# Row sums of a softmax: eight probability tiles added on GpSimd, and one group of narrow matmuls fewer

## The reference, cut to what is computed

```python
def one_block(qblk):
    s = jnp.einsum('bqkgd,bskd->bkgqs', qblk, k).astype(jnp.float32) * scale
    p = jax.nn.softmax(s, axis=-1).astype(v.dtype)
    return jnp.einsum('bkgqs,bskd->bqkgd', p, v)
```

## Time and profile before

| what | value |
|---|---|
| median of 3 runs | 3239.37 us (3236.63 to 3240.04) |
| span of the profiled execution | 3236.2 us |
| mean granted TensorE clock | 0.973 |
| TensorE busy | 3079.7 us (95%) |
| VectorE busy | 1814.2 us (56%) |
| ScalarE busy | 992.9 us (31%) |
| GpSimd busy | 414.4 us (13%) |
| additions on GpSimd (L709) | 96 |
| narrow matmuls, records on L2025 | 1048 |

### The profile page before, as it was taken

How to read it: one execution, slowest core, us unless ns; L and a number is a source line. 1 busy time by engine, 2 the same in 40 slices (tenths; PEclk the granted TensorE clock), 3 DMA queues, 4 the chain that set the end, 5 groups by cost and what they waited for, 6 DMA issues and landing times.

```text
span 3236.2 us, 44976 instructions
## 1 busy us (share of the span) xinstructions
PE 3079.7 (95%) x17016; PEld 2535.1 (78%) x17016; DVE 1814.2 (56%) x3358; ACT 992.9 (31%) x1913; POOL 414.4 (13%) x605
## 2 busy tenths in 40 slices
PE   5999979999999999999979999899989999999998
PEld 4788855567888888889968888555679998899987
DVE  4446677755745444544475376777457445544457
ACT  3223235435311121112253223444352212122212
POOL 0012333311000000000020023343110000000002
PEclk7999989999999999999999999899999999999999
DMA  5430220002322222221112102200121101101111
GB/s 219 154 126 29 79 78 0 0 27 77 94 70 87 74 83 73 84 79 66 36 62 77 54 16 77 78 0 0 32 82 60 53 27 53 52 27 53 40 40 72
DMA packets 94507, 201.25 MB, mean 62 GB/s; under 512 B 13041, under 2 KB 13681, under 8 KB 93809
## 3 DMA queue, kind: packets, MB, share of 16 engines
q1 hardware_dynamic: 78240, 151.76, 14.8%
q0 software_dynamic: 16080, 46.96, 4.2%
HBM read 181.59 MB, written 17.08 MB: 61 GB/s over the span
## 4 chain that ended last, share of the span: by engine, by line
PE 62%; issue 24%; DVE 7%; DMA 2%; ACT 2%; DVEq 1%; POOL 1%; ACTq 1%; POOLq 0%; SPq 0%
PE ps L1805 15%; PE ps L1808 14%; PE ps L1809 14%; PE ps L2025 6%; PE ps L1996 3%; PE ps L2015 2%; PE ps L2016 2%; PE ps L1787 1%; DVE nm L1509 1%; DMA w_raw<-in_w_slots 1%; PE ps L1923 1%; DVE w_lo L499 1%; DMA modw<-in_w_mod 1%; PE ps L1918 1%; DMA w_raw<-in_m_slots 1%
## 5 line engine op out<-in xcount | busy, mean ns | idle before, releaser
L1805 PE MATMUL ps<-hi,w_hi 128*128 128x384 f32 x1584 | 540.4, 341 | 21.8 <-DVEq L437 9.9
L1809 PE MATMUL ps<-hi,w_lo 128*128 128x384 f32 x1584 | 534.0, 337 | 0.0
L1808 PE MATMUL ps<-lo,w_hi 128*128 128x384 f32 x1584 | 533.6, 337 | 0.0
L494 ACT CAST w_hi<-w_raw 128x512 fp32r<-128x512 f32 x368 | 213.8, 619 | 767.8 <-PE ps L1805 720.3
L1805 PE MATMUL ps<-w_hi,hi 128*128 128x512 f32 (+1 forms) x1008 | 389.4, 386 | 7.3 <-ACT stg L810 4.1
L1808 PE MATMUL ps<-w_lo,hi 128*128 128x512 f32 (+1 forms) x1008 | 381.3, 378 | 0.0
L1809 PE MATMUL ps<-w_hi,lo 128*128 128x512 f32 (+1 forms) x1008 | 381.3, 378 | 0.0
L1668 DVE TENSOR_TENSOR ps<-ps,gate 128x512 f32<-128x512 f32 x288 | 201.0, 698 | 261.4 <-PE ps L1809 261.0
L1805 PE MATMUL ps<-w_hi,f_hi 128*128 128x512 f32 x864 | 342.6, 397 | 0.0
L1808 PE MATMUL ps<-w_lo,f_hi 128*128 128x512 f32 x864 | 337.0, 390 | 0.0
L1809 PE MATMUL ps<-w_hi,f_lo 128*128 128x512 f32 x864 | 336.6, 390 | 0.0
(11 more groups left out here) (299 smaller groups left out, 4758.5 us busy)
## 6 DMA issues: line engine op xcount, KB each, us to landing
w_raw<-in_w_slots SPq DMA_DIRECT2D x368, 256.0 KB, 3.4
w_raw<-in_m_slots SPq DMA_DIRECT2D x160, 256.0 KB, 2.8
out<-xr POOLq DMA_DIRECT2D x18, 512.0 KB, 3.2
modw<-in_w_mod SPq DMA_DIRECT2D x4, 2048.0 KB, 15.8
acc<-in_x_in SPq DMA_DIRECT2D x3, 1536.0 KB, 22.6
zq_dram<-stg POOLq DMA_DIRECT2D x18, 256.0 KB, 2.4
xr<-in_x_in POOLq DMA_DIRECT2D x2, 2304.0 KB, 9.3
xr<-out POOLq DMA_DIRECT2D x2, 2304.0 KB, 9.8
```

The costliest lines, as they stand in the source:

```text
L494: act.copy(w_hi[:, j, :], w_raw[:, j % RAW, :]).then_inc(S["w_hi_done"], 1)
L1805: mm = pe.matmul(out, a_hi, b_hi, start=first, stop=False)
L1808: pe.matmul(out, a_hi, b_lo, start=False, stop=False)
L1809: return pe.matmul(out, a_lo, b_hi, start=False, stop=last)
```

## The change

- GpSimd adds tiles 0 to 7 into `psm`, seven additions a step in place of three (`SUMS` = 7). Additions 1 to 4 stand ahead of the four diagonals one by one, 5 to 7 behind the last diagonal.
- `row_sums` is gone. `ninth` now holds the ones with `psm` on rows 0 to 31, the ones with tile 8 on rows 32 to 63, and the ninth tile's values on rows 64 to 127. So there are 5 groups of side matmuls for each step in place of 6.
- `ninth` waits for the seventh addition, and stands after score product 2, not directly behind pair 3.
- `outputs_T` stands after score product 4 in place of 3, so behind scores 2. `sums_T` stays after product 5, turns 64 rows to 64 columns a head, and has one semaphore increment more.
- ScalarE copies values and sums after exponential 2 in place of 1, both after `ninth`, and the sums as 64 rows.
- Exponentials wait for the addition that reads their tile, and for fewer groups of side matmuls (`FREED`).
- VectorE adds two parts of the sum in place of four. At the prompt's tokens two matmuls with ones are made in place of four.

```diff
-PASSES = 6
-FREED = (1, 1, 2, 2, 6, 6, 6, 5, 5)
+PASSES = 5
+FREED = (1, 1, 2, 2, 3, 3, 4, 4, 5)
+SUMS = NT - 2
...
-                        if nk > 1 and h < 3:
+                        if nk > 1:
                             added(h + 1)
                         if nn:
                             diagonal(G, g, h)
+                    for k in range(HG + 1, SUMS + 1) if nk > 1 else ():
+                        added(k)
...
                     act.wait_ge(S["st_ps"], E + j + 1)
-                    if j == 0:
+                    if pk == NT and j < NT - 1:
+                        act.wait_ge(S["sum_done"], START + A - SUMS + max(j, 1))
+                    elif j == 0:
                         act.wait_ge(S["sum_done"], START + A)
...
-                    act.wait_ge(S["pv_done"], START + B - 1)
+                    act.wait_ge(S["pv_done"], START + B)
                     act.copy(o_s[:], ps[:, 5, :]).then_inc(S["o_cp"], n)
...
-                    act.copy(sm_s[:], ps[:, 6, :]).then_inc(S["sm_cp"], n)
+                    act.copy(sm_s[0:HD], ps[0:HD, 6, :]).then_inc(S["sm_cp"], n)
...
-                        if pk > 1 and j == min(1, nk - 1):
+                        if pk > 1 and j == min(2, nk - 1):
                             values_out(G - 1, B)
                             sums_out(G - 1, B)
...
-                    s4 = ps[:, 6, :].rearrange("p (a b c) -> p a b c", b=4, c=32)[:, :, :, 0]
+                    s4 = ps[:, 6, :].rearrange("p (a b c) -> p a b c", b=4, c=32)[:, :, 0:2, 0]
...
-                def ninth(G, E, g):
+                def ninth(G, E, A, g):
 
                     pe.wait_ge(S["ex_done"], START + E + NT)
                     pe.wait_ge(S["oy_done"], START + G)
-                    side(0, 32, 5, vst[:, g, 8, 0:32], pr[:, 8], False, True)
-                    side(32, 32, 5, vst[:, g, 8, 32:HD], pr[:, 8], False, True)
-                    side(64, 32, 6, ones[:, 0:32], pr[:, 7], True, False)
-                    side(96, 32, 6, ones[:, 0:32], pr[:, 8], True, False).then_inc(S["pv_done"], 1)
-
-                def row_sums(A, g):
-
-                    pe.wait_ge(S["sum_done"], START + A + 3)
+                    pe.wait_ge(S["sum_done"], START + A + SUMS)
                     side(0, 32, 6, ones[:, 0:32], psm[:, g], True, True)
-                    side(32, 32, 6, ones[:, 0:32], pr[:, 4], True, True)
-                    side(64, 32, 6, ones[:, 0:32], pr[:, 5], False, True)
-                    side(96, 32, 6, ones[:, 0:32], pr[:, 6], False, True).then_inc(S["pv_done"], 1)
+                    side(32, 32, 6, ones[:, 0:32], pr[:, 8], True, True)
+                    side(64, 32, 5, vst[:, g, 8, 0:32], pr[:, 8], False, True)
+                    side(96, 32, 5, vst[:, g, 8, 32:HD], pr[:, 8], False, True).then_inc(S["pv_done"], 1)
...
                     pe.wait_ge(S["sm_cp"], START + G + 1)
+                    own(pe)
                     for h in range(HG):
-                        mm = pe.transpose(ps[:, 6, h * P:(h + 1) * P], sm_s[:, h * P:(h + 1) * P], ident[:])
+                        mm = pe.transpose(ps[:, 6, h * P:h * P + HD], sm_s[0:HD, h * P:(h + 1) * P], ident[0:HD, 0:HD])
...
                         if pk > 1 and j == min(1, nk - 1):
                             pairs(G - 1, e1, 1 - g, 3)
-                            ninth(G - 1, e1, 1 - g)
-                            row_sums(a1, 1 - g)
-                        if pk > 1 and j == min(3, nk - 1):
+                        if pk > 1 and j == min(2, nk - 1):
+                            ninth(G - 1, e1, a1, 1 - g)
+                        if pk > 1 and j == min(4, nk - 1):
                             if nn:
                                 pe.wait_ge(S["q_lo_done"], START + G + 2)
                             outputs_T(G - 1)
```

More of the change, by code:

```diff
@@ L64 @@
 PREP = ((0, 1), (), (2,), ())
-PASSES = 6
-FREED = (1, 1, 2, 2, 6, 6, 6, 5, 5)
+PASSES = 5
+FREED = (1, 1, 2, 2, 3, 3, 4, 4, 5)
+SUMS = NT - 2
 N_P = 2 * NS * PASSES + 2
-N_A = 2 * NS * 3
+N_A = 2 * NS * SUMS
 START = 8
@@ L444, in counts @@
                 return (NG * L + 2 * NS + g, N_E * L + 2 * NS * NT + g, N_P * L + 2 * NS * PASSES,
-                        N_A * L + 2 * NS * 3)
+                        N_A * L + 2 * NS * SUMS)
             return (NG * L + 2 * t + g, N_E * L + 2 * NT * t + NT * g, N_P * L + 2 * PASSES * t + PASSES * g,
-                    N_A * L + 6 * t + 3 * g)
+                    N_A * L + 2 * SUMS * t + SUMS * g)
         def walk(eng, L, step, between=None):
@@ L2031, in pairs @@
                     pe.wait_ge(S["ex_done"], START + E + 2 * i + 2)
-                    side(0, HD, 5, vst[:, g, 2 * i], pr[:, 2 * i], i == 0, False)
-                    side(HD, HD, 5, vst[:, g, 2 * i + 1], pr[:, 2 * i + 1], i == 0, i == 3).then_inc(S["pv_done"], 1)
-                def ninth(G, E, g):
+                    side(0, HD, 5, vst[:, g, 2 * i], pr[:, 2 * i], i == 0, i == 3)
+                    side(HD, HD, 5, vst[:, g, 2 * i + 1], pr[:, 2 * i + 1], i == 0, False).then_inc(S["pv_done"], 1)
+                def ninth(G, E, A, g):
                     pe.wait_ge(S["ex_done"], START + E + NT)
                     pe.wait_ge(S["oy_done"], START + G)
-                    side(0, 32, 5, vst[:, g, 8, 0:32], pr[:, 8], False, True)
-                    side(32, 32, 5, vst[:, g, 8, 32:HD], pr[:, 8], False, True)
-                    side(64, 32, 6, ones[:, 0:32], pr[:, 7], True, False)
-                    side(96, 32, 6, ones[:, 0:32], pr[:, 8], True, False).then_inc(S["pv_done"], 1)
-                def row_sums(A, g):
-                    pe.wait_ge(S["sum_done"], START + A + 3)
+                    pe.wait_ge(S["sum_done"], START + A + SUMS)
                     side(0, 32, 6, ones[:, 0:32], psm[:, g], True, True)
-                    side(32, 32, 6, ones[:, 0:32], pr[:, 4], True, True)
-                    side(64, 32, 6, ones[:, 0:32], pr[:, 5], False, True)
-                    side(96, 32, 6, ones[:, 0:32], pr[:, 6], False, True).then_inc(S["pv_done"], 1)
+                    side(32, 32, 6, ones[:, 0:32], pr[:, 8], True, True)
+                    side(64, 32, 5, vst[:, g, 8, 0:32], pr[:, 8], False, True)
+                    side(96, 32, 5, vst[:, g, 8, 32:HD], pr[:, 8], False, True).then_inc(S["pv_done"], 1)
                 def values_last(G, E):
@@ L2059, in values_last @@
                     side(HD, HD, 5, vst[:, 1, NT], pr[:, 1], True, True).then_inc(S["pv_done"], 1)
-                    for j in range(4):
-                        mm = side(32 * j, 32, 6, ones[:, 0:32], pr[:, j % 2], True, True)
+                    for j in range(2):
+                        mm = side(32 * j, 32, 6, ones[:, 0:32], pr[:, j], True, True)
                     mm.then_inc(S["pv_done"], 1)
@@ L2078, in step @@
                     G, E, B, A = counts(L, t, g)
-                    e1, a1 = E - pk, A - (3 if pk > 1 else 0)
+                    e1, a1 = E - pk, A - (SUMS if pk > 1 else 0)
                     for j in range(nk):
```

## The result

The changed kernel is slower. Its median is 3254.66 us (3251.53 to 3259.97) beside 3238.9 us for the kernel before on the same chip: ratio 1.0056, interval 1.0043 to 1.0068. That is 15.8 us more, and outside the range on record, which ended at 3251. One run of e3, of 10493.66 us, was slow; it is in neither the median nor the ratio given for e3.

What follows compares the result with a forecast made beforehand. Maximum 1 was taken to bound TensorE ahead of scores 2, TensorE itself from there to the shift. Steady steps +5.6 and layer ends -3.6 gave +2.0 us: 3241.4 us, own range 3235.6 to 3247, 8 in 10 3230 to 3251.

Steps and rivals of the forecast that it cites:

- The bound: Steady step: scores 2 wait for maximum 1, so removing a 0.86 us group ahead of them gains only 0.22 us.
- Rival 1: Whole kernel: TensorE is the bound throughout, so all 27.4 us come back, 3212 us; chance 0.10.
- The moved transposes: Outputs' transposes, moved from the wait ahead of scores 2 to behind them: +0.49 us a steady step.
- rival 2: Scores 2 to shift: unseen slack makes moved transposes cost less, 0.4 us less a steady step, 3231.8 us; chance 0.10.
- The 64-row transposes: Sums' transposes behind scores 2: -0.19 us for smaller size, +0.15 for the way in and out of column tiles.
- Rival 3: Drains around new tiles: 64-row transposes gain nothing, pay 0.15 us twice; steady step +0.57, 3249.5 us; chance 0.25.
- The steady sum: Steady step: -0.22 + 0.49 - 0.19 + 0.15 = +0.23 us, times 24 = +5.6; bounds +0.05 and +0.40 a step.
- GpSimd in steady steps: Seven additions fit: diagonal 3 done 0.6 us ahead of the shift, add 7 about 3 us ahead of the ninth; cost 0.
- the second query part (0.3): VectorE's second query operations, under the other additions: 0.3 us of cover, so no cost.
- The ends of a layer: Prompt steps closing each layer: -0.6, -0.9 and -0.3 us, together -1.8 a layer, -3.6 in all.
- The splits of w_lo under additions may take half of it: VectorE's weight splits at the layer ends: slowed by additions, they may halve the -3.6 us gain; bounds -1.6 to -5.
- rival 4: TensorE's clock falls in the new waits: each 10 us at 1.2 GHz costs about 5, several falls 3260 us; chance 0.05.

Runs made afterwards that it cites:

- e3: Changed kernel with GpSimd additions 4 to 7 left out, so three a step: 3243.85 us, ratio 1.0023 to the kernel before.
- e5: Changed kernel with three additions, ninth directly behind pair 3, copies after exponential 1, outputs' transposes after product 3: 3233.84 us, ratio 0.9983 to the kernel before.
- e2: Kernel before with only the outputs' transposes moved from after score product 3 to after product 4: 3248.21 us, ratio 1.0034.
- e11: Changed kernel with additions 4 to 7 left out and the outputs' transposes back after product 3: 3237.28 us, ratio 0.9994 to the kernel before.
- e6: Changed kernel with VectorE's w_lo splits moved behind the maxima of the last two prompt steps: 3246.94 us, ratio 1.0025 to the kernel before.
- e12: Changed kernel with the outputs' transposes back after product 3 and addition 4 alone left out: 3240.75 us, ratio 1.0008 to the kernel before.
- e4: Changed kernel with only the outputs' transposes back after score product 3, ahead of scores 2: 3253.03 us, ratio 1.0054 to the kernel before.
- e1: Kernel before with four more GpSimd additions a step on a scratch tile, placed as in the changed kernel: 3242.08 us, ratio 1.0017.
- e9: e4 and e6 together, with VectorE's query copy written as a two-input maximum: 3252.36 us, ratio 1.0044 to the kernel before.
- e10: e8 and e9 together: 3272.7 us, ratio 1.0103 to the kernel before.
- e8: e4 and e6 together, with addition 4 put behind diagonal 3 as well: 3270.75 us, ratio 1.0107 to the kernel before.

## Why the prediction was wrong

- *The bound.* Right. Scores 2 wait for maximum 1, and the removed group, 27.4 us of TensorE, gives only what lies ahead of that wait: forecast 0.22 a step; the loop's first part became 0.24 shorter (4.61 and 4.87 in place of 4.97 and 4.99), and in e5 scores 2 come 0.26 earlier. Rival 1 (3212 us) is dead: e5, with little else changed, is at 3233.84.
- *The moved transposes.* Right in place, a little too dear: 0.39 in e2 and 0.45 in the changed kernel (from scores 2 to the shift 6.40 in e3 and 5.95 in e11) in place of 0.49. So rival 2, with no cost left, did not come.
- *The 64-row transposes.* Forecast -0.04. The pitch from their start to the next product is 0.39 (552.00 to 552.39), as it was with 128 rows, 0.38, and from the second matmul of the product ahead of them to the product behind it is 0.70 (551.69 to 552.39) in place of 0.62 (538.06 to 538.68). So +0.08. From scores 2 to the shift it is +0.09 (5.95 in e11, 5.86 before). The term -0.19, taken from the 36-row ones, was wrong: half the rows bought nothing. The Trainium skill, TensorEngine Tiling (Array Packing), Key Properties, says a change of tiling mode drains the array; the trace agrees in sign, with this 0.08 beside it. Rival 3 had its mechanism here, but with 0.30 for these transposes, 0.57 a step, it was far too dear. Slower had a chance of 0.30 in all, and most of the miss came by a way that no rival named. TensorE before, the second matmul of the product ahead of the transposes:

```profile
538.06 0.40 PE L2016 MATMUL ps<-q_lo,kst 128*128 128x512 f32 x1
```

- *The steady sum.* +0.23 forecast, +0.33 measured, inside the bounds of 0.05 to 0.40: -0.24 ahead of scores 2, +0.54 behind it (6.40 in place of 5.86), +0.03 behind the shift. The 0.54 is 0.09 for the 64-row transposes and 0.45 for the moved ones. In e2 these cost only 0.39, because the 128-row transposes of the sums, with the product behind them, became 0.06 shorter there: 538.80 to 539.70 in e2, 538.30 to 539.26 before. In 24 steps this is 2.3 us of the miss.
- *GpSimd in steady steps.* Its timetable was right: the shift never waits for diagonal 3, and addition 7 is ahead of the ninth. But the cover of "the second query part (0.3)" was wrong: addition 4 makes the copy take 1.22 us in place of 0.33 (L1470 before, at 539.87), 0.9 more. The prediction missed that the queries' transposes wait for the outputs behind this copy. It cost only 0.07 in the changed kernel, because the moved transposes had lengthened TensorE's run by as much; without them it costs 0.40.
- *The ends of a layer.* **This step failed.** Forecast -0.6, -0.9 and -0.3, measured -0.42, +2.27 and +0.26 in layer 1. "The splits of w_lo under additions may take half of it" was the term that was mis-sized: at most 2.0 us of gain lost, over both layers. Additions 4 to 7 took 6.0 there, by the changed kernel less e3: 2.45 and 0.45 in layer 1, 2.66 and 0.45 in layer 2. Two things stand on one chain in (7,1). 0.8 us on each of four splits stood ahead of the prompt's maxima, for which diagonal 0 and all that follows it were waiting; e6 takes this away and brings 2.17. And addition 4 stood ahead of diagonal 3; e12 takes this away and brings 1.68 beside e4. The two do not add, since TensorE's own work takes 12.33. e1 makes 1.53 of the loss without the rest of the change. A second part of the miss is gains that did not come: without the four additions (e3) the three steps give -0.42, -0.18 and -0.19, so -0.8 a layer in place of -1.8. The ends give +4.3 where -3.6 stood in the sum: 7.9 of the 10.2 us by which the attention steps miss.
- *Around the steps.* The rest of the span is 1.2 us longer (13.5 - 12.25). I took the 3.2 us between span and median as fixed; the median lies 5.0 above the span here (3254.66 - 3249.7). That is 1.8 more; no profile shows the median execution, so it stays open. With the 10.2 and the 1.2 us this is the whole miss of 13.3.
- *The clock (rival 4).* The stretch 545.30 to 560.02 of the kernel after, columns as in rows 2:

```profile
545.30:560.02 14.72, 13.94 (x69) 7.50 (x71) 11.23 (x18) 7.08 (x14) 10.83 (x11) 1.00 0.00 0
```

It stays at 1.00, the level of 2.4 GHz, though TensorE is now idle 0.78 us of the step in place of 0.08. Over 447 to 670 and 2070 to 2290 us it is 1.00 and 0.99, before 0.99 and 1.00. The new waits cost no clock.

The range was too narrow because the bounds of that one term, taken as half of a gain, did not admit a loss. That it could be a loss could have been read from the trace of before: one addition makes L1448 take 1.00 in place of 0.41, and four splits (658.95) stood where three new additions were to come, straight ahead of the maxima (662.21).

## What to carry to other kernels

Cost idle time on a slow engine by what it meets: for each added GpSimd operation list the VectorE operations that start under it and have both inputs in SBUF or copy from SBUF to SBUF, take the rest of the GpSimd operation as the price of each, and then ask what stands behind them in VectorE's queue. Where undoing either of two parts gives nothing, undo both before you clear them: two chains of nearly equal length hide each other. Work taken from an engine that is busy 95% is worth nothing as far as it lies ahead of a wait; find the wait first.

## What the runs showed of the hardware

A VectorE operation with both inputs in SBUF, or a copy from SBUF to SBUF, that starts under a GpSimd addition does not run at half speed: it ends just after the addition does. The copy of e4, which takes 0.29 us alone, ends 0.14 us after addition 4 (570.62 and 570.48); the two-input form of e9, 0.42 alone in e10, ends 0.28 after it (558.52 and 558.24); L1453 of e8 ends 0.29 after its addition (568.69 and 568.40). The operations here that read PSUM are not held. The maximum takes its 1.36 us beside an addition that starts with it, VectorE and GpSimd after:

```profile
550.74 1.36 DVE L1514 TENSOR_REDUCE nm<-ps 128x1 f32<-128x1152 f32 x1 [0.88 <-PE ps L2001]
...
550.74 1.28 POOL L710 TENSOR_TENSOR psm<-psm,pr 128x512 f32<-128x512 f32 x1 [0.20 <-ACT pr L972]
```

The additions wait in turn when they come second: 1.46 to 1.71 us beside the splits in place of 1.28. The Trainium skill, SBUF — State Buffer, section SBUF: two separate sides, says this: of a GpSimd operation and a VectorE operation that has two SBUF inputs or runs in a two-port mode, the one that starts first locks the port pair that both engines share, for the whole of it. These rows agree. The prediction had read rows 7 as a slowdown and had not looked at where the operation ends, 0.3 us after the addition. By that rule the price is the rest of an addition for each meeting, up to 1.3 us. An addition with one tile as both inputs (e1) took 1.04 us where one with two tiles took 1.28. And four transposes of 64 rows to 64 columns took as long as four of 128 to 128 in this place, 0.39 and 0.38 us.
